# A weight sum moved from VectorE to an adding DMA, M5 ahead of M7 in each Strassen-Winograd group, and the third merge group spread over its block

## What is computed

```python
merged = jax.nn.sigmoid(g_a) * (y_a @ w_up_a[i]) + jax.nn.sigmoid(g_b) * (y_b @ w_up_b[i])
x = x + merged @ w_o[i]
h = rmsnorm_2(x, ffn_norm_g[i])
hid = h @ w_ffn_in[i]                                    # 2048 -> 2 x 5632
x = x + (jax.nn.silu(hid[..., :FFN_HIDDEN]) * hid[..., FFN_HIDDEN:]) @ w_ffn_out[i]
```

## Time and profile before

| | |
|---|---|
| median of 3 executions | 1987.65 us (1985.18, 1987.65, 1987.70) |
| the profiled execution, its device time | 1987.31 us |
| its span in the profile | 1985.5 us |
| TensorE busy | 1975.6 us |
| VectorE busy | 1476.5 us |
| ScalarE busy | 1147.4 us |
| bytes moved by DMA | 535.95 MB |
| mean granted TensorE clock | 0.999 of full |

### The profile page before, as it was taken

One profiled execution on the slowest core, in us unless ns is written; L12 is line 12 of the kernel. 1 busy time (PEld: TensorE's weight loads), 2 busy tenths in 40 slices (PEclk: granted clock), 3 DMA queues, 4 the chain that ended last, 5 costly groups with the idle time before them and its releaser, 6 DMA issues.

```text
span 1985.5 us, 23547 instructions
## 1 busy us (share of the span) xinstructions
PE 1975.6 (100%) x9126; PEld 1644.4 (83%) x9126; DVE 1476.5 (74%) x1571; ACT 1147.4 (58%) x1417; POOL 116.0 (6%) x140
## 2 busy tenths in 40 slices
PE   9999999999999999999999999999999999999999
PEld 8888888888888888888887888888888888888887
DVE  6877776555666666768888657888988888888764
ACT  7546444554466456556765445666666666666553
POOL 2000010000001110000000000000000000000000
PEclk9999999999999999999999999999999999999999
DMA  9788798999889998857797786788878887877553
GB/s 377 253 251 276 233 323 274 330 324 311 282 284 308 335 336 293 258 208 249 282 297 240 296 239 237 239 304 273 272 231 305 266 266 240 309 247 238 208 179 124
DMA packets 86815, 535.95 MB, mean 270 GB/s; under 512 B 10416, under 2 KB 11184, under 8 KB 40752
## 3 DMA queue, kind: packets, MB, share of 16 engines
q1 hardware_dynamic: 72736, 458.69, 61.3%
q0 software_dynamic: 13824, 75.50, 19.8%
q10 hardware_dynamic: 144, 0.26, 0.0%
HBM read 529.69 MB, written 105.38 MB: 320 GB/s over the span
## 4 chain that ended last, share of the span: by engine, by line
PE 96%; DVE 2%; DMA 1%; ACT 1%; issue 0%; DVEq 0%; ACTq 0%
PE acc L1342 45%; PE acc L1347 23%; PE aux L1699 15%; PE aux L1703 7%; PE aux L1325 1%; PE aux L1415 1%; DMA ple<-in_w_in 1%; DVE wlo L1851 1%; DVE wlo L2507 1%; PE aux L1780 0%; DVE ple L2502 0%; DMA x_stage<-in_x_gain_and_columns 0%; PE aux L1405 0%; PE aux L1430 0%; DVE att_z L2353 0%
## 5 line engine op out<-in xcount | busy, mean ns | idle before, releaser
L1851 DVE TENSOR_TENSOR wlo<-raw,whi 128x1024 fp32r<-128x1024 f32 x512 | 624.1, 1225 | 357.6 <-ACT whi L915 348.4
L915 ACT ACTIVATE whi<-raw 128x1024 fp32r<-128x1024 f32 x511 | 537.7, 1059 | 539.1 <-PE acc L1347 499.4
L1342 PE MATMUL acc<-whi,actA_hi 128*128 128x512 f32 x892 | 352.6, 395 | 0.0
L1342 PE MATMUL acc<-whi,actA_lo 128*128 128x512 f32 x892 | 348.2, 390 | 0.0
L1342 PE MATMUL acc<-whi,actB_hi 128*128 128x512 f32 x796 | 312.7, 393 | 0.2 <-DVE actB_lo L2624 0.2
L1342 PE MATMUL acc<-whi,actB_lo 128*128 128x512 f32 x796 | 309.9, 389 | 0.0
L1164 ACT ACTIVATE whi<-ple 128x1024 fp32r<-128x1024 f32 x192 | 202.3, 1060 | 141.7 <-PE acc L1347 89.1
L2507 DVE TENSOR_TENSOR wlo<-ple,whi 128x1024 fp32r<-128x1024 f32 x192 | 232.0, 1222 | 40.2 <-ACT whi L1164 33.6
L1347 PE MATMUL acc<-wlo,actA_hi 128*128 128x512 f32 x892 | 238.7, 389 | 0.0
L1347 PE MATMUL acc<-wlo,actB_hi 128*128 128x512 f32 x796 | 213.2, 390 | 0.7 <-DVE wlo L1851 0.6
L2507 DVE TENSOR_TENSOR wlo<-raw,whi 128x1024 fp32r<-128x1024 f32 x144 | 175.3, 1222 | 35.1 <-ACT whi L1164 29.8
(11 more groups left out here) (360 smaller groups left out, 2394.1 us busy)
## 6 DMA issues: line engine op xcount, KB each, us to landing
raw<-in_w_in SPq DMA_DIRECT2D x108, 1024.0 KB, 7.4
raw<-in_w_ffn_out SPq DMA_DIRECT2D x44, 1024.0 KB, 6.8
summed<-in_w_ffn_in POOLq DMA_DIRECT2D x36, 1024.0 KB, 11.1
raw<-in_w_ffn_in SPq DMA_DIRECT2D x72, 512.0 KB, 7.6
ple<-summed SPq DMA_DIRECT2D x24, 1024.0 KB, 4.7
raw<-summed SPq DMA_DIRECT2D x48, 512.0 KB, 4.8
ple<-in_w_ffn_in SPq DMA_DIRECT2D x18, 1024.0 KB, 7.5
ple<-in_w_ffn_in POOLq DMA_DIRECT2D x36, 512.0 KB, 9.6
```

The lines of the kernel that those rows point to most:

```text
L915: act.activation(whi[:, g % RING], raw_piece(g), ACT.Copy).then_inc(hi_ready, 1)
L1342: pe.matmul(acc2(n)[:, t, :], act[x][:, k + c, t * P:(t + 1) * P], whi[:, g % RING, c, :], start=(p == 0 and c == 0 and x == 0), stop=False)
L1851: dve.tensor_tensor(wlo[:, g % RING], raw_piece(g), whi[:, g % RING].bitcast(F32), ALU.subtract)\
```

## The change

M6's weights are now made as M4's are: GpSimd issues an adding DMA of b22 into `r1[q]` when the low part of M5's piece q has been made, four per group, ahead of the four for M4; `s_sum` and its semaphore go. M5 stands ahead of M7 in each group. b22 is now loaded for M3 alone, so its load is asked for at M3.q. In merge group 2 the divisor is len(std) - 1 in place of len(std) - 3, which puts four S pieces after each standard piece and leaves none behind M4; the first of the transposes behind it moves from the second to the third piece.

```diff
--- before.py
+++ after.py
@@ -86,7 +86,7 @@
 MERGE_LAST = [("uA", 3), ("uB", 3)]
 MERGE_S = [1, 2, 3]
 M_GROUPS = len(MERGE_S)
-MERGED_AT = (1, 4, 6)
+MERGED_AT = (2, 4, 6)
 BLOCKS = [
     (1, [("gB", 0), ("uB", 0, 0, 0, 2)]),
     (2, [("uB", 0, 0, 2, 4), ("uA", 1), ("uB", 1)]),
@@ -110,9 +110,8 @@
 HID_S = [0, 1, 0, 2, 1, 0, 2, 1, 0]
 OUT_LAST = 10
 S_GROUPS = len(BLOCKS)
-S_ORDER = [(m, q) for m in ("M1", "M2", "M7", "M5") for q in range(4)] \
+S_ORDER = [(m, q) for m in ("M1", "M2", "M5", "M7") for q in range(4)] \
     + [("M6", 0), ("M6", 1), ("M3", 0), ("M6", 2), ("M3", 1), ("M6", 3), ("M3", 2), ("M3", 3)] + [("M4", q) for q in range(4)]
-S_LEAD = 2
 
 
 SUM_STEP = 5.2
@@ -215,7 +214,7 @@
         for t, x in enumerate(std):
             self.after[c, t] = self.g
             self.add_std(x, 2)
-            upto = max(0, min(28, t * 28 // (len(std) - 3)))
+            upto = max(0, min(28, t * 28 // (len(std) - (1 if c == M_GROUPS - 1 else 3))))
             while done < upto:
                 self.add_s(c, done)
                 done += 1
@@ -261,10 +260,10 @@
                 self.loads.append((free, self.s_at[c, "M1", 2 * h], "r1", h, c))
                 self.loads.append((self.s_at[c, "M1", 2 * h + 1], self.s_at[c, "M5", 2 * h], "fifth", h, c))
             for i, (m, q) in enumerate(S_ORDER):
-                for what, first, last in (("b21", "M2", "M2"), ("b22", "M6", "M3"), ("seventh", "M7", "M7")):
+                for what, first, last in (("b21", "M2", "M2"), ("b22", "M3", "M3"), ("seventh", "M7", "M7")):
                     if m == first:
                         slot = RAW // 2 + n % 4
-                        need = at(i - S_LEAD if m == "M6" else i)
+                        need = at(i)
                         self.loads.append((self.last_use[slot], need, "half", slot, (c, what, q)))
                         self.half[c, what, q] = (slot, 16 * (n // 4 + 1))
                         self.last_use[slot] = self.s_at[c, last, q]
@@ -508,9 +507,7 @@
             return raw[:, slot]
 
         S_SRC = {"M1": None, "M2": "b21", "M5": None, "M6": None, "M7": "seventh", "M3": "b22", "M4": None}
-        S_ADDEND = {"M6": "b22"}
-        S_DMA = {"M4": ("b21", "M6")}
-        S_SUMS = [x for x in S_ORDER if x[0] in S_ADDEND]
+        S_DMA = {"M6": ("b22", "M5"), "M4": ("b21", "M6")}
         S_BANK = {"M5": 1, "M3": 1, "M7": 2}
         S_FORM = {"M5": 0, "M6": 1, "M7": 2, "M3": 3}
 
@@ -527,13 +524,9 @@
 
             return r1[:, q] if S_SRC[m] is None else half_slot(c, S_SRC[m], q)
 
-        def s_summed(eng, c, m, q):
-
-            eng.wait_ge(sem("s_sum"), c * len(S_SUMS) + S_SUMS.index((m, q)) + 1)
-
         def r1_added(eng, c, m, q):
 
-            eng.wait_ge(sem(f"r1_added{q}"), 16 * (c + 1))
+            eng.wait_ge(sem(f"r1_added{q}"), 16 * (2 * c + (1 if m == "M6" else 2)))
 
         def s_weights(c, what, q):
 
@@ -1156,8 +1149,6 @@
                     act.wait_ge(sem(f"r1_loaded{q // 2}"), 32 * c + (16 if m == "M1" else 32))
                 elif m in S_DMA:
                     r1_added(act, c, m, q)
-                elif m in S_ADDEND:
-                    s_summed(act, c, m, q)
                 else:
                     half_loaded(act, c, S_SRC[m], q)
                 act.wait_ge(piece_used, g - RING + 1)
@@ -2495,12 +2486,6 @@
                             lo_split(AUX[("yaT", i)], actA, 2 * i)
 
 
-            def s_sum(c, m, q):
-
-                half_loaded(dve, c, S_ADDEND[m], q)
-                x = s_source(c, m, q)
-                dve.tensor_tensor(x, x, half_slot(c, S_ADDEND[m], q), ALU.add).then_inc(sem("s_sum"), 1)
-
             def s_lo(g, c, m, q):
 
                 dve.wait_ge(hi_ready, g + 1)
@@ -2557,8 +2542,6 @@
                 else:
                     c, i, m, q = x
                     s_lo(g, c, m, q)
-                    if i + S_LEAD < 28 and S_ORDER[i + S_LEAD] in S_SUMS:
-                        s_sum(c, *S_ORDER[i + S_LEAD])
                 t = g - PLAN.g_plan
                 if t == 4:
                     slab_taken(dve, FIRST["E2"] - 1)
```

## The result

Median of 9 executions 1990.88 us (1989.06 to 1995.99), against 1987.65 for 9 of the kernel before: ratio 1.002, 95% interval 1.0011 to 1.003. So it is slower by some 3 us, where a gain of 3 us, to 1984.4, was forecast. The profiled execution took 1989.06 us.

The account below looks back on a forecast made before the run. TensorE's work was taken as the floor, with one hole to win; -4.2 for it, +0.3 new VectorE wait and +0.7 wait for M4.3's add made -3.2, from the median 1987.65 to 1984.4 us; range 1982.0 to 1993.0.

Parts of the forecast that it names:

- the DMA case: Rival, chance 0.19: DMA engines become the bound, M4.3 late in ten groups from a pace of 4.3 us: 2004 us.
- the hole of 4.2 us: TensorE's lost time at M4.3 in group 2, waiting plus slower matmuls, 4.21 us; the sum takes it as -4.2.
- The 2.08 us of slower matmuls: Part of the loss at M4.3 in group 2: after the wait the granted clock is 0.67 of full.
- VectorE had no lead left: At M6.3 in group 2 VectorE was 0.3 us behind TensorE; taking its sums away returns 2.7 us.
- No gain of its own: Spreading group 2 wins nothing by itself, as the distance from M6.3 to M4.3 stays 10.9 us.
- M6's adds: Four new adds per group, landing within 18.9 us of the first issue, none late for its piece: cost 0.
- 1.2 us to spare: In GpSimd's queue, M4's first add would land at 24.2, while the queue could land it at 23.0.
- the reserve of 3.1 us: Slower chain each group bears: 1.2 us in the queue plus M4.3's own 1.9 us from group 6.
- b22's move: Load of b22 for M3.0, now beside adds, takes at most 9.2 us and is in time by 2.7.
- VectorE's products: Two products of slab uB 2 come between M4.0 and M4.3 in group 2: 0.3 us of new wait.
- Sums off VectorE: Removing 58.5 us of VectorE sums, hidden behind TensorE everywhere but at M4.3 in group 2, is directly worth 0.
- The rule of the page DMA: Bandwidth & Descriptors: Fit for one GpSimd DMA, about 2.0 us plus bytes: 3.2 us per add, sum 1983.4; the rows were kept instead.

Follow-up runs that it names:

- e15: The kernel before, unchanged, profiled again; it lost 3.0 us in group 2 over the profile of the spread alone.
- e1: Only the spread of merge group 2 and its transposes one piece later, on the kernel before; 1985.49 us against 1987.27, ratio 0.9994.
- e9: The spread alone on the kernel before, run a second time; 1985.07 us against 1987.13, ratio 0.9988.
- e10: The changed kernel without M6's adds and without the spread, so the third merge group is as dense as before; 1988.13 us, ratio 1.0004.
- e17: The kernel before without VectorE's 48 sums, M6 computed with M5's weights; group 2 lost 1.8 us at M4.3.
- e18: The kernel before without VectorE's 48 sums, run once more; group 2 lost 1.4 us at M4.3.
- e5: The changed kernel, unchanged, run again; 1989.09 us, ratio 1.0012 to the kernel before.
- e6: The changed kernel without M6's 48 adding DMAs, M6 computed with M5's weights; 1984.19 us, ratio 0.9988.
- e12: The changed kernel with M7 ahead of M5 again and all adds kept; 2015.05 us in one execution.
- e3: The changed kernel with M6.0 to M6.3 all ahead of M3.0 to M3.3; 1988.16 us, ratio 1.0004.
- e2: The changed kernel without the spread, the third merge group and its transposes as before; 1993.08 us, ratio 1.0028.

## Why the prediction was wrong

The time went the other way than forecast. It lies inside the stated range only because a mild form of the DMA case, which the forecast held to be unlikely, set the range's upper end. (That end has 8.6 us for ten groups late by 0.4 us and as much again for the clock; these make 8.0.)

- *The sum's first term, the hole of 4.2 us.* Read rightly from its rows, but from one execution. Four lose 3.6, 1.1, 1.7 and 3.0 us over the spread alone. The 2.08 us of slower matmuls came in one of the four: e15 waited longer and its clock stayed at 1.00. What the spread had to win was 2.3 us on the mean, and the medians of e1 and e9 won 1.8 and 2.1.
- *Why the hole is there.* "VectorE had no lead left" was true (the lead is back, 2.86 us at M6.3, as forecast at 2.7) and worth at most some 0.7 us (e10, e17, e18). "No gain of its own" for the spread was wrong, since I measured the distance from M6.3 to M4.3, 10.9 us in either case. The chain starts at M6.0, and from there to M4.3 it is 17.7 us in the dense group and 20.4 in the spread one: 2.7 us of room that I put at nothing.
- *M6's adds.* They landed 18.3 to 20.0 us after the first issue in groups 0 to 10, forecast 18.9, and all adds landed 6.8 us or more ahead of TensorE's start of their pieces. Right.
- ***The step that failed:* "1.2 us to spare" and the reserve of 3.1 us.** I let M4.0's add start when the queue was free and gave it the 7.6 us of before. It took 9.1 to 10.8. The followers mostly kept their pace (in group 3 of e5 3.8, 3.9 and 3.8 us), but in group 2 two were slower (4.7 and 5.0). M4.3's add thus landed 37.0 to 39.1 us after the first issue, where 35.3 was forecast and 37.4 was the limit; by TensorE's starts the limit was 37.6 in group 2 and 37.9 to 38.7 in the others. Of the 3.1 us only the 1.9 were there for M4's own adds: the 1.2 are a gap in the queue ahead of them. From M4.0's issue to M4.3's landing it took 21.5 us at the median where 18.9 was assumed, 2.6 more. The two causes, b22's loads in new company and M6's adds, are each small; I had costed b22's move only for its own punctuality (it is in time, as I said) and not for what it does to the adds beside it.
- *The DMA rival.* It had the mechanism, M4.3 late in many groups, and a share of the DMA engines of 0.94 in group 6 (I gave 0.99). But it was tied to a pace of 4.3 us throughout and to M6's adds landing later than 22 us; neither came. The upper end of the range, ten groups late by 0.4 us, was nearest to what happened.
- *VectorE's products,* 0.3: 0.46 in the spread alone. *Sums off VectorE,* 0: right; no engine gained by it, as e1 and e6 end up within their intervals of each other.
- *The rule of the page DMA: Bandwidth & Descriptors* in the Trainium skill (section Anatomy of one DMA) gave an estimated 3.2 us for an add. The changed kernel's took 6.0 to 14.8, and even end to end (e12) one took 4.0; the measurement decides. Its section on queues, rings and completion order has the engines taking turns between queues; in line with that, loads and adds slowed one another (13.3 for 8.9 us, 9.6 for 7.6).

## What to carry to other kernels

When transfers run one behind another in one queue, count the time to the last one from the issue of the first and against the consumer of the last, not from the last one's own issue; and even that count holds only while the loads beside them stay the same (in e17 and e18 the first was issued some 2 us sooner and the last landed no sooner). When a load moves, ask whom it slows, not only whether it is in time. And before a hole of a few microseconds becomes the first term of a sum, look at it in more than one execution: this one varied from 1.1 to 3.6.

## What the hardware showed unexpectedly

- The length of a wait does not foretell the clock behind it. After 1.96 us of idle time it was 0.67 and after 1.98 in e3 0.66, but after 2.93 in e15 it stayed at 1.00. (After 3.10 in e2, with 0.76 idle 5 us earlier, it was 0.50.) The windows behind M4.3 of group 2, of e3 and of e15:

```profile
1080.00:1085.00 5.00, 4.96 (x15) 3.95 (x16) 4.40 (x4) 5.00 (x6) 0.00 (x0) 0.66 0.29 76
```

```profile
1074.80:1080.00 5.20, 5.08 (x21) 3.88 (x22) 5.14 (x5) 5.05 (x7) 0.00 (x0) 1.00 0.13 27
```

- M4.0's add took 7.6 us before, 8.9 to 9.3 with b22's loads beside it, and 9.5 to 9.6 with M6's adds before it as well, of which the last landed 2 to 4 us after its issue.
- The stretch ahead of group 0, the same code in all, took 893.4 to 899.9 us. In e1's it was one window (700 to 800 us) with TensorE busy for 96.66 us at a clock of 0.97, in e9's 99.90 at 1.00. With scatter of that size, ten executions a side tell two microseconds apart only just.
